# Attention's reciprocal row sums: through DRAM and back as one row, in place of diagonals and a product with ones

## The chip, the cores and the metric

One core of one Trainium2 chip runs the whole program, with its five engines: TensorE (PE), VectorE (DVE), ScalarE (ACT), GpSimd (POOL) and SyncE (SP), the last of which here only issues DMAs. The metric is the device time of one launch in microseconds. Three runs of the kernel before took 2953.47, 2957.74 and 2959.49 us; their median is 2957.74 us.

## What is computed

Two layers over x (2048 tokens of width 1024, float32). The even layer has a gated linear attention branch and a latent attention branch (MLA), the odd layer a gated MLP. The change touches only the end of MLA:

```
s = einsum('bqhd,bkhd->bhqk', qn_i, kn) + einsum('bqhr,bkr->bhqk', qr_i, kr)
p = softmax(s, axis=-1)
o = einsum('bhqk,bkhd->bqhd', p, v)
return o * silu(z)                 # 4 heads, 2048 queries, values of 128
```

The kernel doesn't divide p. It computes exp(s - max), multiplies by the values, and applies 1 / (row sum) together with silu(z) at the end. The values' product is held transposed (value dimension on partitions, queries along the free axis), so the 256 reciprocals of a pair of query tiles, computed as one number per partition, have to become a row that all 128 partitions hold.

## The kernel before, in words

MLA takes 4 heads x 16 tiles of 128 queries. A step I (32 of them) is a pair of tiles u = 0, 1; N = 2I + u numbers the tiles. All engines run the same sequence of steps written out by hand, with counting semaphores between them; nothing is reordered at run time.

- PE (`attn_pe`, L1767). `scores(N)` writes four banks of 512 keys, five matmuls each (L1775 to L1779). `turn(N, c)` transposes a quarter of exp(s) (8 transposes for two calls, L1786) and may write its bank only when DVE has read what the bank held before (the wait on `s_lo`). `values(I, c)` is 16 times a pair of matmuls (L1808, L1809). In step I, u = 0: scores of tile 2I with turns 0 and 1 of the tile before between banks 1 and 2, then turns 2 and 3, then the first half of the values of step I-1. For u = 1: the scores of tile 2I+1, with turns 0 and 1 of tile 2I between, then `shares(I-1)`, the second half of the values of step I-1, turns 2 and 3.
- DVE (`attn_dve`, L1944). Per tile: four maxima (L1947), their maximum (L1950), its negative times the scale (L1952, the tile `nm`), four low parts of the turned exp(s) (L1965), the row sum (L1958), its reciprocal (L1960, tile `rinv`), and one sum for the next layer's modulation (L1746), which reads a piece of `wmod` that SP loaded into `mw`. Once a step also `shared` (L1971), which multiplies the reciprocals' row into the gate tile `mzt`, and `outs` (L1977, L1978, L1980).
- ACT (`attn_act`). Four exponentials per tile (L1889, they wait for `nm`) and four high parts (L1896, they wait for the turns).
- POOL (`attn_pool`, L2046). `diagonal` makes diag(rinv) in three instructions (L2054, L2056, L2058); it waits for `rinv` and for `shares` of the step before. `query_split` (three instructions) then makes the parts of the queries two tiles ahead.
- SP (`attn_sp`). Per step: for each u the queries of two tiles ahead (L1445, L1447 twice; they wait for POOL's split), the `wmod` piece (L1738), then the store of the step before (L2084) and the gate tile (L2079).

`shares` on PE multiplies a matrix of ones with the high and the low part of the two diagonals, two matmuls of 256 columns into bank 7 (L1795, L1796); DVE reads the row from there. After the last step come the remaining turns, the modulation products (`mod1_pe`), the last `shares` and the last values; SP goes on with loads for the output projection.

Of the kernel before, what the change touches and what calls it, by code (L numbers as in the profile page):

```python
# [18 lines left out]
F32 = mybir.dt.float32  # L19
# [5 lines left out]
ds = bass.ds  # L25
# [42 lines left out]
def emit(nc, a, out):  # L68
# [5 lines left out]
    mixT = scratch("mixT", (KD, P, S))  # L74
    q_all = scratch("q_all", (P, MH * S))
    q_rot = scratch("q_rot", (ROPE, MH * S))
    x1 = scratch("x1", (S, D))
    gla_vs = scratch("gla_vs", (NT, P, GH * DV + 2 * DV))
    gla_a = scratch("gla_a", (NT, P, GH, P))
# [4 lines left out]
    with ExitStack() as ctx:  # L84
# [1563 lines left out]
        mvl = at("mvl", M0 + 32 * K, [P, MH, S], F32R)  # L1648
        pb_ = at("pb_", M0 + 111 * K, [P, 2, S])
        pt = at("pt", M0 + 127 * K, [P, NT, 2, 2 * P], F32R)  # L1650
        dgh = at("dgh", M0 + 64 * K, [P, 2, P], F32R)
        dgl = at("dgl", M0 + 65 * K, [P, 2, P], F32R)
        qraw = at("qraw", M0 + 68 * K, [P, 2, 2, P])
        qsl = at("qsl", M0 + 76 * K, [P, 2, 3, P], F32R)
        diag = at("diag", M0 + 168 * K, [P, 2, P])
        mzt = at("mzt", M0 + 169 * K, [P, 2 * P])
        ost = at("ost", M0 + 170 * K, [P, 2 * P])
        mx4 = at("mx4", M0 + 171 * K, [P, 2, 4])
# [40 lines left out]
        s_nm = sem("s_nm")  # L1699
        s_exp = sem("s_exp")  # L1700
        s_rinv = sem("s_rinv")
        s_dg = sem("s_dg")
        s_T = sem("s_T")
        s_hi = sem("s_hi")
        s_lo = sem("s_lo")
# [61 lines left out]
        def attn_pe(pe):  # L1767
# [19 lines left out]
                                      ident[:, :])  # L1787
                mm.then_inc(s_T, 1)

            def shares(I):  # L1790

                pe.wait_ge(s_dg, I * 6 + 12)
                pe.wait_ge(s_rz, I + 1)
                both = ones[:, :].bitcast(F32R)
                pe.matmul(PS[:, 7, 0:2 * P], both, dgh[:, :, :].rearrange("p u c -> p (u c)"), start=True, stop=False)  # L1795
                pe.matmul(PS[:, 7, 0:2 * P], both, dgl[:, :, :].rearrange("p u c -> p (u c)"), start=False, stop=True  # L1796
                          ).then_inc(s_rb, 1)

            def values(h, I, c):

                vh, vl = mvh[:, h, :], mvl[:, h, :]
# [10 lines left out]
            def step(h, i):  # L1812
                I = i + h * NP_
                first = isinstance(i, int) and i == 0
                opening = h == 0 and first
                hb = h - 1 if first else h
                for u in range(2):
                    N = i * 2 + (h * NT + u)

                    def turn_if(c):  # L1820
                        if u or not opening:
                            turn(N - 1, 1 - u, c)

                    def values_if(c):
                        if not opening:
                            values(hb, I - 1, c)

                    def pieces(*ns):
                        if opening:
                            for n in ns:  # L1830
                                piece_pe(pe, n)
                    if opening and u == 0:
                        pe.wait_ge(s_mor, NT - 1)
                        scores(h, N, u, (0,))
                        pieces(0, 1)
                        pe.wait_ge(s_mor, NT)
                        scores(h, N, u, (1,))
                        pieces(2)
                        pe.wait_ge(s_mgz, NT)
                    else:  # L1840
                        scores(h, N, u, (0, 1))
                    turn_if(0)
                    turn_if(1)
                    if u:
                        pieces(8, 9)
                    scores(h, N, u, (2,))
                    if u:
                        pieces(10, 11)
                    else:
                        pieces(3)  # L1850
                    scores(h, N, u, (3,))
                    if u == 0:
                        turn_if(2)
                        turn_if(3)
                        values_if(0)
                        values_if(1)
                        pieces(*range(4, 8))
                    else:
                        if not opening:
                            shares(I - 1)  # L1860
                        pieces(12, 13)
                        values_if(2)
                        values_if(3)
                        turn_if(2)
                        turn_if(3)
                        pieces(14, 15)
# [6 lines left out]
            for p in range(2):  # L1873
                for c in (2 * p, 2 * p + 1):
                    turn(MH * NT - 1, 1, c)
                if p:
                    mod1_pe(pe)
                    shares(MH * NP_ - 1)
                values(MH - 1, MH * NP_ - 1, 2 * p)
                if p:  # L1880
                    mod1_last(pe)
                values(MH - 1, MH * NP_ - 1, 2 * p + 1)
# [61 lines left out]
        def attn_dve(dve):  # L1944
# [7 lines left out]
                    dve.tensor_scalar(nm[:, u:u + 1], mx1[:, u:u + 1], rq2[:, 0, ds(i * 2 + u, 1)], -1.0, ALU.mult, ALU.mult  # L1952
                                      ).then_inc(s_nm, 1)

            def sums(N, u):
                dve.wait_ge(s_exp, N * 4 + 8)
                dve.wait_ge(s_dg, N * 3 + 1)
                dve.tensor_reduce(rsm[:, u:u + 1], rs4[:, u, :], AX, ALU.add).then_inc(s_rinv, 1)  # L1958
                dve.wait_ge(s_rinv, N * 2 + 1)
                dve.reciprocal(rinv[:, u:u + 1], rsm[:, u:u + 1]).then_inc(s_rinv, 1)  # L1960
# [5 lines left out]
                                  pt[:, o[0], 0, o[1]].bitcast(F32), ALU.subtract).then_inc(s_lo, 1)  # L1966

            def shared(I):
                dve.wait_ge(s_rb, I + 2)
                dve.wait_ge(s_mlg, I * 16 + 16)  # L1970
                dve.tensor_tensor(mzt[:, :], PS[:, 7, 0:2 * P], mzt[:, :], ALU.mult).then_inc(s_rz, 1)  # L1971

            def outs(I):
                dve.wait_ge(s_rz, I + 2)
# [7 lines left out]
            def step(h, i):  # L1982
                I = i + h * NP_
                opening = h == 0 and isinstance(i, int) and i == 0
                for u in range(2):
                    N = i * 2 + (h * NT + u)

                    def lo(c):
                        if u or not opening:
                            los(N - 1, 1 - u, c)  # L1990

                    def pieces(*ns):
                        if opening:
                            for n in ns:
                                piece_dve(dve, n)
                    maximum(N, i, u, 0)
                    if u == 0:
                        pieces(0, 1)
                    maximum(N, i, u, 1)
                    lo(0)  # L2000
                    lo(1)
                    if u:
                        pieces(8, 9)
                    else:
                        pieces(2)
                    maximum(N, i, u, 2)
                    if u == 0:
                        pieces(3)
                        maximum(N, i, u, 3)
                        lo(2)  # L2010
                        lo(3)
                        pieces(*range(4, 8))
                    else:
                        pieces(10, 11)
                        maximum(N, i, u, 3)
                        if not opening:
                            shared(I - 1)
                        pieces(12, 13)
                        if not opening:
                            outs(I - 1)  # L2020
                        lo(2)
                        lo(3)
                        pieces(14, 15)
                    sums(N, u)
                    mod1_sum(dve, h, i, u)
            heads(dve, step)
            for c in range(4):
# [18 lines left out]
        def attn_pool(pool):  # L2046
            def split(N, I, u):
                query_split(pool, N, I, u)

            def diagonal(N, I, u):  # L2050
                pool.wait_ge(s_rinv, N * 2 + 2)
                pool.wait_ge(s_rb, I + 1)
                pool.wait_ge(s_dg, N * 3 + 6)
                pool.tensor_tensor(diag[:, u, :], ident[:, :], rinv[:, u:u + 1].broadcast_to([P, P]), ALU.mult).then_inc(s_dg, 1)  # L2054
                pool.wait_ge(s_dg, N * 3 + 7)
                pool.tensor_tensor(dgh[:, u, :], diag[:, u, :], zero[:, 0:1].broadcast_to([P, P]), ALU.add).then_inc(s_dg, 1)  # L2056
                pool.wait_ge(s_dg, N * 3 + 8)
                pool.tensor_tensor(dgl[:, u, :], diag[:, u, :], dgh[:, u, :].bitcast(F32), ALU.subtract).then_inc(s_dg, 1)  # L2058

            mod1_start(pool)  # L2060
            with pool.Fori(0, MH * NP_ - 1) as I:
                for u in range(2):
                    diagonal(I * 2 + u, I, u)
                    split(I * 2 + 2 + u, I + 1, u)
            for u in range(2):
                diagonal(MH * NT - 2 + u, MH * NP_ - 1, u)

        def attn_sp(sp):
            for u in range(2):
# [7 lines left out]
            def gates(h, i, I):  # L2077
                sp.wait_ge(s_oe, I + 1)
                sp.dma_start(mzt[:, :], projT[h + T_MZ, :, ds(i * (2 * P), 2 * P)]  # L2079
                             ).then_inc(s_mlg, 16)  # L2080

            def store(h, i, I):
                sp.wait_ge(s_oe, I + 2)
# [3 lines left out]
            def step(h, i, last):  # L2087
# [8 lines left out]
                elif h:  # L2096
                    store(h - 1, NP_ - 1, I - 1)
                gates(h, i, I)
            mod1_rows(sp)
            for h in range(MH):  # L2100
                step(h, 0, False)
# [998 lines left out]
        def _(pool):  # L3100
# [6 lines left out]
            pool.sem_inc(s_q, 6)  # L3107
            main_pool(pool)

            pool.sem_inc(s_dg, 6)  # L3110
            attn_pool(pool)

            out_pool(pool, 0, lambda: (norm_pool_front(pool, 4), norm_pool_front(pool, 5)))
# [41 lines left out]
        def _(pe):  # L3155
# [4 lines left out]
            pe.sem_inc(s_S, 8)  # L3160
            pe.sem_inc(s_T, 8)
            pe.sem_inc(s_O, 4)
            pe.sem_inc(s_rb, 1)

            attn_pe(pe)

# [75 lines left out]
```

## Time and profile before

| | |
|---|---|
| median of three runs | 2957.74 us (2953.47 to 2959.49) |
| profiled execution: its own time, its span | 2955.36 us, 2953.6 us |
| mean granted TensorE clock | 0.988 |
| PE busy | 2878.6 us (97%) |
| DVE busy | 1597.1 us (54%) |
| ACT busy | 1351.9 us (46%) |
| POOL busy | 1101.2 us (37%) |
| MLA's 32 steps in the span | about 745 to 1360 us |

Busy is the share of time in which at least one instruction of the engine is in flight. Matmuls overlap, so on PE the distance from one start to the next says what a matmul costs, and "busy" doesn't show short waits. The span runs from the first to the last instruction; 1.8 us of the execution's time lie around it.

### The profile page before, as it was taken

What the parts mean: (1) busy time and instruction counts of PE and PEld (TensorE: products, weight loads), DVE (VectorE), ACT (ScalarE), POOL (GpSimd) and SP (SyncE); (2) the same over time, 40 slices, a digit from 0 to 9 for tenths busy, and PEclk for the clock granted to TensorE, in tenths of its full rate; (3) what the DMA queues carried; (4) which work ended last, traced back from release to release, by engine and by line L of the source; (5) the groups of instructions that cost most, each with busy time, mean ns of one, the idle gap of its engine ahead of it and who ended that gap; (6) DMA issues with size and microseconds to landing.
All of it is one profiled execution on the core that took longest, in us unless ns stands there. A gap on an engine that the chain in (4) does not pass through costs nothing.

```text
span 2953.6 us, 48956 instructions
## 1 busy us (share of the span) xinstructions
PE 2878.6 (97%) x16038; PEld 2398.2 (81%) x16038; DVE 1597.1 (54%) x2745; ACT 1351.9 (46%) x2444; POOL 1101.2 (37%) x1085
## 2 busy tenths in 40 slices
PE   7999999999999999999999999999999999999998
PEld 6768888788788888887877888888887888888887
DVE  5567777766777777773435222255557554532111
ACT  4652254565555555553235111265657665632111
POOL 0211111223233333332321762086766777623221
PEclk8999999989999999999999999999999999999999
DMA  7243355587111122123643332333235332244321
GB/s 282 61 131 102 103 164 159 164 286 255 59 57 55 56 57 57 57 58 134 192 163 122 136 150 85 103 126 103 96 103 185 108 103 99 99 158 150 104 95 57
DMA packets 279082, 356.88 MB, mean 121 GB/s; under 512 B 22116, under 2 KB 186084, under 8 KB 278407
## 3 DMA queue, kind: packets, MB, share of 16 engines
q1 hardware_dynamic: 273576, 339.45, 35.6%
q0 software_dynamic: 3072, 11.54, 1.0%
q10 hardware_dynamic: 2304, 4.20, 0.4%
q8 instruction: 77, 1.26, 0.2%
q14 instruction: 53, 0.43, 0.0%
HBM read 241.20 MB, written 111.80 MB: 120 GB/s over the span
## 4 chain that ended last, share of the span: by engine, by line
PE 87%; DVE 4%; ACT 3%; issue 2%; DMA 2%; POOL 1%; SPq 0%; DVEq 0%; ACTq 0%; POOLq 0%
PE PS L3028 6%; PE PS L3032 6%; PE PS L3036 6%; PE PS L2387 4%; PE PS L2389 4%; PE PS L2388 4%; PE PS L366 4%; PE PS L368 4%; PE PS L367 4%; PE PS L1808 4%; PE PS L1786 4%; PE PS L2555 4%; PE PS L2557 4%; PE PS L2556 4%; PE PS L1809 2%
## 5 line engine op out<-in xcount | busy, mean ns | idle before, releaser
L366 PE MATMUL PS<-hTh,whi 128*128 128x512 f32 x640 | 258.1, 403 | 1.5 <-DVE hTl L320 1.1
L3028 PE MATMUL PS<-hTh,wc 128*128 128x512 f32 x896 | 243.9, 394 | 8.0 <-DVE zu L2962 5.0
L368 PE MATMUL PS<-hTh,wlo 128*128 128x512 f32 x640 | 250.7, 392 | 0.0
L367 PE MATMUL PS<-hTl,whi 128*128 128x512 f32 x640 | 250.6, 392 | 0.0
L1889 ACT ACTIVATE pb__159<-PS,nm,rq 128x512 f32<-128x512 f32 x256 | 197.3, 779 | 106.5 <-DVE nm L1952 106.3
L2784 POOL TENSOR_TENSOR wc<-wpr,wc 128x512 fp32r<-128x512 f32 x128 | 176.9, 1382 | 179.3 <-ACT wc L2780 179.3
L3032 PE MATMUL PS<-hTh,wc 128*128 128x512 f32 x896 | 240.4, 390 | 0.0
L3036 PE MATMUL PS<-hTl,wc 128*128 128x512 f32 x896 | 239.8, 389 | 0.0
L2387 PE MATMUL PS<-ow_h,of_h 128*128 128x512 f32 x576 | 224.3, 389 | 1.4 <-DVE oy L2338 1.4
L2388 PE MATMUL PS<-ow_l,of_h 128*128 128x512 f32 x576 | 224.1, 389 | 0.0
L2389 PE MATMUL PS<-ow_h,of_l 128*128 128x512 f32 x576 | 224.1, 389 | 0.0
L2334 DVE SCALAR_TENSOR_TENSOR oy<-PS,small,gate 128x1024 f32<-128x1024 f32 x32 | 41.1, 1284 | 329.3 <-POOL small L2309 329.3
L1896 ACT ACTIVATE pt<-PS 128x512 fp32r<-128x512 f32 x256 | 139.4, 598 | 152.5 <-PE PS L1786 152.5
L2555 PE MATMUL PS<-vsh,hTh 128*128 128x512 f32 x512 | 199.8, 390 | 2.0 <-DVE vsl L2505 1.5
L3028 PEld LDWEIGHTS PS<-hTh,wc 128*128 128x128 f32 x896 | 165.9, 188 | 42.8 <-issue 10.3
L2557 PE MATMUL PS<-vsh,hTl 128*128 128x512 f32 x512 | 199.2, 389 | 0.0
L2556 PE MATMUL PS<-vsl,hTh 128*128 128x512 f32 x512 | 199.2, 389 | 0.0
L3032 PEld LDWEIGHTS PS<-hTh,wc 128*128 128x128 f32 x896 | 168.8, 188 | 35.4
L3036 PEld LDWEIGHTS PS<-hTl,wc 128*128 128x128 f32 x896 | 168.2, 188 | 35.6 <-DVE hTl L2728 0.6
L1808 PE MATMUL PS<-pt,mvh 128*128 128x512 f32 x512 | 185.8, 402 | 1.1 <-DVE pt L1965 1.1
L2054 POOL TENSOR_TENSOR diag<-ident,rinv 128x128 f32<-128x128 f32 x64 | 38.3, 598 | 395.6 <-PE PS L1796 284.1
L2301 POOL TENSOR_TENSOR of_l<-of,of_h 128x1024 fp32r<-128x1024 f32 (+1 forms) x24 | 84.4, 3517 | 240.2 <-ACT of_h L2262 240.2
(303 smaller groups left out, 7052.5 us busy)
## 6 DMA issues: line engine op xcount, KB each, us to landing
wpr<-wuz SPq DMA_DIRECT2D x128, 256.0 KB, 3.3
xt<-x SPq DMA_DIRECT2D x8, 2048.0 KB, 8.8
mw<-wmod SPq DMA_DIRECT2D x64, 256.0 KB, 2.7
oxt<-x SPq DMA_DIRECT2D x32, 512.0 KB, 4.9
sg_v<-vev SPq DMA_DIRECT2D x64, 256.0 KB, 2.4
vm<-sg_v SPq DMA_DIRECT2D x32, 512.0 KB, 3.8
sgT<-mT SPq DMA_DIRECT2D x32, 512.0 KB, 3.5
chnk<-pev SPq DMA_DIRECT2D x48, 256.0 KB, 2.7
```

The lines of the kernel that those rows point to most:

```text
L366: pe.matmul(PS[:, bank, :], w[1][:, s, k, :], hTh[:, k, b], start=(k == 0), stop=False)
L367: pe.matmul(PS[:, bank, :], w[1][:, s, k, :], hTl[:, k, b], start=False, stop=False)
L368: mm = pe.matmul(PS[:, bank, :], w[2][:, s, k, :], hTh[:, k, b], start=False, stop=(k == KD - 1))
L2387: pe.matmul(o, w["fh"][:, u, k, :], w["h"][:, k, c], start=(k == 0), stop=False)
L2388: pe.matmul(o, w["fh"][:, u, k, :], w["lo"][:, k, c], start=False, stop=False)
L2389: mm = pe.matmul(o, w["fl"][:, u, k, :], w["h"][:, k, c], start=False, stop=(k == OK[l] - 1))
L2555: pe.matmul(o, hTh[:, k, tok], vsh[:, k, :], start=(k == 0), stop=False)
L2556: pe.matmul(o, hTh[:, k, tok], vsl[:, k, :], start=False, stop=False)
L2557: mm = pe.matmul(o, hTl[:, k, tok], vsh[:, k, :], start=False, stop=(k == KD - 1))
L3028: pe.matmul(o, wc[:, k, 0, kk, :], h_tile(hTh, k, kk), start=(kk == 0 and not onto), stop=False, skip_group_check=onto)
L3032: pe.matmul(o, wc[:, k, 1, kk, :], h_tile(hTh, k, kk), start=False, stop=False, skip_group_check=onto)
L3036: mm = pe.matmul(o, wc[:, k, 0, kk, :], h_tile(hTl, k, kk), start=False, stop=(kk == 3), skip_group_check=onto)
```

## The change

POOL's `diagonal` and PE's `shares` go, with the tiles `diag`, `dgh`, `dgl`. SP stores `rinv` (128 partitions x 2 numbers) into a row of 256 numbers in DRAM, waits for that store, and loads the row into all 128 partitions of a new tile `share`. The row's order is (q u), so `shared` on DVE reads `share` with a step of two numbers. DVE's row sum waits until the store of the step before has read `rinv`.

```diff
+    rinvd = scratch("rinvd", (MH + 1, NT * P))
...
-        dgh = at("dgh", M0 + 64 * K, [P, 2, P], F32R)
-        dgl = at("dgl", M0 + 65 * K, [P, 2, P], F32R)
+        share = at("share", M0 + 64 * K, [P, 2 * P])
-        diag = at("diag", M0 + 168 * K, [P, 2, P])
...
-            def shares(I):
-                pe.wait_ge(s_dg, I * 6 + 12)
-                pe.wait_ge(s_rz, I + 1)
-                both = ones[:, :].bitcast(F32R)
-                pe.matmul(PS[:, 7, 0:2 * P], both, dgh[...], start=True, stop=False)
-                pe.matmul(PS[:, 7, 0:2 * P], both, dgl[...], start=False, stop=True).then_inc(s_rb, 1)
...
-                        if not opening:
-                            shares(I - 1)
...
-                    shares(MH * NP_ - 1)
...
-            def sums(N, u):
+            def sums(N, I, u):
                 dve.wait_ge(s_exp, N * 4 + 8)
-                dve.wait_ge(s_dg, N * 3 + 1)
+                if not isinstance(I, int) or I:
+                    dve.wait_ge(s_rst, I * 16)
...
             def shared(I):
-                dve.wait_ge(s_rb, I + 2)
+                dve.wait_ge(s_rb, I * 16 + 16)
                 dve.wait_ge(s_mlg, I * 16 + 16)
-                dve.tensor_tensor(mzt[:, :], PS[:, 7, 0:2 * P], mzt[:, :], ALU.mult).then_inc(s_rz, 1)
+                mz = mzt[:, :].rearrange("p (u q) -> p u q", u=2)
+                dve.tensor_tensor(mz, share[:, :].rearrange("p (q u) -> p u q", u=2), mz, ALU.mult).then_inc(s_rz, 1)
...
-            def diagonal(N, I, u):
...
                 for u in range(2):
-                    diagonal(I * 2 + u, I, u)
                     split(I * 2 + 2 + u, I + 1, u)
...
+            def row_shares(h, i, I):
+                sp.wait_ge(s_rinv, I * 4 + 4)
+                sp.dma_start(rinvd[h + 1:h + 2, ds(i * (2 * P), 2 * P)].rearrange("a (p u) -> p (a u)", u=2), rinv[:, :]).then_inc(s_rst, 16)
+                sp.wait_ge(s_rst, I * 16 + 16)
+                sp.dma_start(share[:, :], rinvd[h + 1:h + 2, ds(i * (2 * P), 2 * P)].broadcast_to([P, 2 * P])
+                             ).then_inc(s_rb, 16)
...
                 gates(h, i, I)
+                row_shares(h, i, I)
```

## Rows read from the trace of the kernel before

**Rows 1.** Busy time by stretch: us, busy and (count) of PE, PEld, DVE, ACT, POOL, PEclk, DMA share, GB/s

```profile
1000.00:1100.00 100.00, 100.00 (x572) 86.33 (x571) 75.77 (x162) 56.49 (x130) 32.18 (x66) 1.00 0.19 53
```

**Rows 2.** Timeline of PE around `shares`: start us, us, engine, line, operation

```profile
1002.04 0.29 PE L1795 MATMUL PS<-dgh,ones 128*128 128x256 f32 x1
1002.29 0.39 PE L1808 MATMUL PS<-pt,mvh 128*128 128x512 f32 x1
...
1020.60 0.29 PE L1795 MATMUL PS<-dgh,ones 128*128 128x256 f32 x1
```

**Rows 3.** Waits, 780 to 1330 us: who waited for whom, total us, times, longest

```profile
POOL diag L2054 <- PE PS L1796: 274.9, 30, 9.5
...
DVE ost L1977 <- PE PS L1809: 34.9, 27, 1.4
...
DVE mx L1947 <- PE PS L1779: 0.6, 3, 0.2
```

**Rows 4.** Timeline of DVE and ACT over one step

```profile
1003.28 0.22 DVE L1952 TENSOR_SCALAR nm<-mx,rq 128x1 f32<-128x1 f32 x1 [0.15 <-DVE mx L1950]
...
1006.95 0.80 ACT L1889 ACTIVATE pb__159<-PS,nm,rq 128x512 f32<-128x512 f32 x1
...
1007.97 0.16 DVE L1958 TENSOR_REDUCE rsm<-rs 128x1 f32<-128x4 f32 x1
...
1010.13 1.28 DVE L1965 TENSOR_TENSOR pt<-PS,pt 128x512 fp32r<-128x512 f32 x2
...
1011.32 1.28 DVE L1947 TENSOR_REDUCE mx<-PS 128x1 f32<-128x512 f32 x2
...
1012.93 0.21 DVE L1952 TENSOR_SCALAR nm<-mx,rq 128x1 f32<-128x1 f32 x1
...
1015.64 0.78 ACT L1889 ACTIVATE pb__159<-PS,nm,rq 128x512 f32<-128x512 f32 x1
...
1016.64 0.16 DVE L1958 TENSOR_REDUCE rsm<-rs 128x1 f32<-128x4 f32 x1 [2.30 <-ACT pb__159 L1889]
...
1017.12 0.75 DVE L1746 SCALAR_TENSOR_TENSOR macc<-mw,cvec,macc 128x512 f32<-128x512 f32 x1
...
1020.18 1.31 DVE L1947 TENSOR_REDUCE mx<-PS 128x1 f32<-128x512 f32 x2
...
1021.83 0.21 DVE L1952 TENSOR_SCALAR nm<-mx,rq 128x1 f32<-128x1 f32 x1 [0.15 <-DVE mx L1950]
```

**Rows 5.** Timeline of PE: turns 2 and 3 of the odd tile

```profile
1011.47 1.03 PE L1786 MATMUL PS<-ident,pb__159 128*128 128x128 f32 x8
```

**Rows 6.** Timeline of PE: three successive `shares`

```profile
1094.81 0.29 PE L1795 MATMUL PS<-dgh,ones 128*128 128x256 f32 x1
...
1113.44 0.29 PE L1795 MATMUL PS<-dgh,ones 128*128 128x256 f32 x1
...
1131.96 0.29 PE L1795 MATMUL PS<-dgh,ones 128*128 128x256 f32 x1
```

**Rows 7.** Timeline of SP's DMA issues after the end of a step's stores

```profile
1007.28 0.34 SPq L2079 DMA_DIRECT2D mzt<-projT  x1
1008.27 0.33 SPq L1445 DMA_DIRECT2D qraw<-q_all  x1
...
1010.17 0.34 SPq L1738 DMA_DIRECT2D mw<-wmod  x1
```

**Rows 8.** DMA issues, whole span: count, KB each, median us from issue to landing

```profile
mw<-wmod SPq DMA_DIRECT2D x64, 256.0 KB, 2.7
...
mixT<-og SPq DMA_DIRECT2D x16, 256.0 KB, 6.0
...
mixT<-ost SPq DMA_DIRECT2D x32, 128.0 KB, 2.3
```

**Rows 9.** Timeline of PE in the tail, around the last `shares`

```profile
1353.54 1.91 PE L1753 MATMUL PS<-maccg,ones 128*128 128x512 f32 x2
...
1355.46 0.42 PE L1796 MATMUL PS<-dgl,ones 128*128 128x256 f32 x1
```

More of the change, by code:

```diff
@@ L1701, in emit @@
         s_rinv = sem("s_rinv")
-        s_dg = sem("s_dg")
+        s_rst = sem("s_rst")
         s_T = sem("s_T")
@@ L1788, in turn @@
                 mm.then_inc(s_T, 1)
-            def shares(I):
-                pe.wait_ge(s_dg, I * 6 + 12)
-                pe.wait_ge(s_rz, I + 1)
-                both = ones[:, :].bitcast(F32R)
-                pe.matmul(PS[:, 7, 0:2 * P], both, dgh[:, :, :].rearrange("p u c -> p (u c)"), start=True, stop=False)
-                pe.matmul(PS[:, 7, 0:2 * P], both, dgl[:, :, :].rearrange("p u c -> p (u c)"), start=False, stop=True
-                          ).then_inc(s_rb, 1)
             def values(h, I, c):
@@ L2023, in step @@
                         pieces(14, 15)
-                    sums(N, u)
+                    sums(N, i + h * NP_, u)
                     mod1_sum(dve, h, i, u)
@@ L2048, in split @@
                 query_split(pool, N, I, u)
-            def diagonal(N, I, u):
[L2051 to L2058, printed above, removed]
             mod1_start(pool)
@@ L2062, in attn_pool @@
                 for u in range(2):
-                    diagonal(I * 2 + u, I, u)
                     split(I * 2 + 2 + u, I + 1, u)
-            for u in range(2):
-                diagonal(MH * NT - 2 + u, MH * NP_ - 1, u)
         def attn_sp(sp):
@@ L3108, in _ @@
             main_pool(pool)
-            pool.sem_inc(s_dg, 6)
             attn_pool(pool)
@@ L3162, in _ @@
             pe.sem_inc(s_O, 4)
-            pe.sem_inc(s_rb, 1)
             attn_pe(pe)
```

## The prediction, made before the changed kernel ran

> **What bounds the kernel now.** The page first: PE is busy 97% of the span, so an edit that takes two matmuls from each of 32 steps looks like a sure gain. The view by stretches says the same of the place where the edit lies: between 1000 and 1100 us PE is busy 100.00 of 100.00 us, DVE 75.77, ACT 56.49, POOL 32.18 [rows 1]. I don't stop there, because "busy" on PE hides waits shorter than a matmul's flight. The timeline gives PE's real pace: `shares` begins at 1002.04 and the next one at 1020.60, so a step lasts 18.56 us [rows 2].
>
> Then the view of waits. The striking thing is who does not wait: DVE's maxima read PE's scores, and in 550 us they waited for PE three times, 0.6 us in all [rows 3]. If PE alone set the pace, DVE would arrive early at every bank of scores. So I follow DVE and ACT through one step [rows 4]. `nm` of the odd tile starts at 1003.28. ACT's exponentials start from it, back to back with two high parts; the fourth runs at 1006.95, and its accumulator (which comes at the end) frees the row sum at 1007.97. From there DVE goes without a gap: reciprocal, the modulation sum, two maxima, low parts at 1010.13, two maxima at 1011.32, ending with `nm` of the even tile at 1012.93. From 1007.97 to 1012.93 these are eleven DVE instructions, first and last shown; each starts as the one before ends. Then again four exponentials, the fourth at 1015.64, row sum at 1016.64, modulation sum at 1017.12, maxima, low parts, maxima at 1020.18, `nm` at 1021.83. From `nm` to `nm` 18.55 us, the length of the step, and in that ring there is no place where PE is waited for but one: the last maximum at 1020.18 needs the fourth bank of scores. The pair there takes 1.31 us where the pair at 1011.32 takes 1.28. That is all the slack that the ring has: 0.03 us in 18.55.
>
> So two things bind at once: PE's queue at 18.56 and a ring of DVE and ACT at 18.53 that doesn't pass through what is removed. Where PE would meet the ring when it runs ahead: its turn 3 of the odd tile writes a bank that DVE must have read. DVE's low parts that read it end at 1010.13 + 1.28 = 1011.41; PE's turns start at 1011.47, eight of them within 1.03 us, the last ends included, so turn 3 comes near 1011.9 [rows 4, 5]. Less than 0.5 us of lead is open to PE.
>
> A second sign: `shares` at 1094.81, 1113.44 and 1131.96 are 18.63 and 18.52 apart [rows 6]. After a late step PE makes up 0.03 us and not more.
>
> **The change, part by part.**
>
> *PE loses two matmuls a step.* By starts they cost 1002.29 - 1002.04 = 0.25 us [rows 2]. 31 of the 32 stand inside the steps: 31 x 0.25 = 7.75 us of PE's queue. What the time gains is the smaller of this and what the ring allows: 31 x 0.03 = 0.93 us. The rest becomes lead of PE, used up after two steps (2 x 0.25 against at most 0.5), and then a wait of about 0.2 us per step at the turns. Lead that PE still has at the end of the last step buys nothing, because the turns of the last tile wait for the same ring. Bounds: 0 below, 7.75 above; I take 0.9.
>
> One rule speaks of this. The Trainium skill, page "Perfetto Trace Analysis", section "Identifying the Most-Contended Engine", says that matmul busy time doesn't measure how near TensorE is to its limit, and that weight-load busy should be looked at; the rows have 100.00 for the one and 86.33 for the other. By the first view the sum would be the whole 7.75, by the second PE isn't full, as the ring says.
>
> *The last shares* stands in the tail, where PE works without waiting between `mod1_pe` and the last values. `mod1_pe` ends at 1353.54 + 1.91 = 1355.45 and L1796 at 1355.46 + 0.42 = 1355.88 [rows 9]: 0.43 us at most, and 0.25 at the pace of the steps. I take 0.3. DVE's last `shared` gets its row earlier than before; the output's chain still starts from the last values.
>
> *POOL loses six instructions a step.* It waited 274.9 us for PE [rows 3]; nobody waits for POOL in the steps. The query splits come earlier. Worth nothing: bounds 0 and 0.
>
> *DVE's `shared`* reads `share` from SBUF with a step of two numbers instead of PSUM. It runs between `nm` and `outs`, and before `outs` DVE waits for PE's values by 1.3 us (34.9 / 27) [rows 3]. If the read took twice as long, that would still cover it. `nm` is issued ahead of it. Nothing. The row itself arrives some 3 us after the store's landing, where DVE needs it half a step later. The row sum's new wait, for the store of the step before, was met more than half a step earlier, and takes the place of a wait on `s_dg`: nothing.
>
> *SP gets a store, a wait for it, and a load, at the end of each step.* This is the part that can cost. Behind the wait stand, in SP's order, the queries of tile 2I+4 and the `wmod` piece for the even tile. The reciprocals are ready at 1007.97 + 0.16 + 0.16 and gaps = 1008.33; the store issues 0.2 us later, 1008.5. It lands L later; 0.2 more, and the row's load issues at 1008.7 + L. From one issue to the next across the loop's end took 1008.27 - 1007.28 = 0.99 us, and from there to the `wmod` load 1010.17 - 1008.27 = 1.90 [rows 7]. The piece lands 2.7 us after its issue [rows 8]: 1008.7 + L + 0.99 + 1.90 + 2.7 = 1014.3 + L. DVE's modulation sum at 1017.12 [rows 4] has to have it at about 1017.0, and that sum is in the ring. So L may be 2.7 us. The nearest row, `mixT<-ost` with 128 KB, took 2.3 [rows 8]; the new store has 1 KB, in 128 pieces of 8 bytes, and goes behind the gate tile's load in the queue. I take 2.0 to 2.3: margin 0.4 to 0.7 us, cost nothing. The farthest store has 6.0 (`mixT<-og`), as the upper bound. The queries have a whole step of time, and the odd tile's `wmod` piece half a step.
>
> *After the last step* SP's first loads of output weights go out some 3 us later. PE comes to them only behind its last turns, the modulation products and the last values, which start after 1355.88 [rows 9], while SP's loads follow the last reciprocals, ahead of all these: covered, worth nothing.
>
> **Sum.** 0.9 + 0.3 = 1.2 us less. The profiled execution took 2955.36 us and would take 2954.2; it stands 2.38 us below the median, so against the median 2957.74 - 1.2 = 2956.5 us. What a measurement can tell from no change is about 0.2%, 5.9 us.
>
> **The rivals.**
>
> *PE's queue alone sets the pace.* Then 31 x 0.25 + 0.3 = 8.1 us go: 2949.6. For it: PE never shows a wait, 100.00 busy. Against it: the 0.6 us of DVE's waits, and the ring closed in [rows 4]. It would need PE to be ahead at the turns by more than it is. Chance 0.13.
>
> *The `wmod` piece comes late (slower).* If L is over 2.7 us, DVE's modulation sum waits in each step, the ring is longer by L - 2.7, and PE waits with it: 31 x (L - 2.7). With L = 3.1: +12.4 - 0.3, 2969.8; with L = 6.0: +102, 3060. For it: the store is followed by a dependent load on one queue, and margins of half a microsecond rest on medians; the broadcast load lies ahead of the `wmod` load. Against: 1 KB is less than any store in the rows. The Trainium skill, page "DMA: Bandwidth & Descriptors", section "Anatomy of one DMA — SWDGE (gpsimd) path", warns that waiting for a completed write can cause "a surprisingly long delay especially when the write target is HBM"; a fixed cost of about 2.0 us stands there, an estimate by which L would lie inside the margin. Chance 0.19, about 0.05 of it with a loss under 0.2%.
>
> *The ring gets shorter*, because POOL's accesses no longer lie beside DVE's and ACT's. Up to PE's new length, so at most the first rival's time; no row shows DVE slower beside POOL. Chance 0.03.
>
> The forecast has 0.65. Faster by over 0.2%: the 0.13 of the first rival and 0.02 for the third and the spread, 0.15. Slower by over 0.2%: 0.14 of the second and 0.02 for the spread, 0.16. The rest, 0.69, is no difference that can be told. The likeliest case's own range is 2953.5 to 2960, mostly the spread of the runs. The whole range goes to 2949 below and 2966 above.
>
> **What would show it.** Right: steps of 18.52 to 18.54 us between equal PE instructions; late starts of PE at L1786, turn 3 of the odd tile; PE busy no longer 100% in the steps; DVE's `nm` to `nm` unchanged; the modulation sum still right behind the reciprocal in even tiles. Steps of 18.3 us would show the first rival. A wait of DVE's modulation sum for the DMA `mw<-wmod`, and a store of `rinv` that lands later than 2.7 us, would show the second. My forecast is wrong if the ring has slack that I took for work, for one if a step gets clearly shorter than 18.5 us.

## The result, and the profile after

The changed kernel takes 2964.07 us in the median of 20 runs (2958.76 to 2973.49); beside it the kernel before took 2956.14 us in 20 runs (2948.93 to 2962.15). The medians are 7.9 us apart; the ratio is 1.0025, with a 95% interval of 1.0019 to 1.0032, which is 7.4 us slower. Where I say below how many us a kernel gained or lost in time, the figure is worked out from its ratio in the same way, unless I say that it is of steps. I had forecast 1.2 us faster and called it no difference. The time lies inside the range, but on the side of the slower rival, to which I gave 0.19.

The profiled execution of the changed kernel took 2958.76 us, the fastest of its 20. Its span is 2957.0 us, 3.4 more than before. The steps of MLA, from the first `nm` of the phase to the last (from the trace, starts of L1952 and of L1939), took 596.09 us against 591.92, 4.17 more. The rest is -0.8: 1.76 more ahead of the first `nm`, where nothing was changed, 0.69 less from the last `nm` to the output projection, 1.83 less behind that. The parts that the change doesn't touch differ by several us between the profiled executions of the kernels below: the first `nm` comes at 744.5 to 751.1 us, and from the output projection to the end it takes 1588.7 to 1595.8. So I compare the steps; each comparison of them rests on one execution of each kernel.

Busy time by stretch of the kernel after, columns as in [rows 1]. PE, full before, now has short waits:

```profile
1000.00:1100.00 100.00, 99.90 (x555) 83.42 (x554) 74.56 (x159) 56.17 (x128) 19.42 (x34) 1.00 0.28 67
```

The waits of the kernel after, 780 to 1330 us (who waited for whom, total us, times, longest):

```profile
PEld PS L1785 <- DVE pt L1953: 16.4, 70, 0.6
...
DVE macc L1745 <- DMA mw<-wmod: 7.9, 14, 1.4
...
DVE maccg L1745 <- DMA mw<-wmod: 2.5, 6, 0.8
```

None of the three lines exists before the change. The modulation sum waits for its `wmod` piece in 20 steps, always in the even tile, 10.4 us in all (`macc` is its accumulator in the first three heads, `maccg` in the fourth; some 0.13 us of each wait is there in steps without a late piece too), and PE's turns wait for DVE's low parts behind it. SP's own waits in the same stretch show what the piece stands behind:

```profile
SPq L2062 <- DMA rinvd<-rinv: 71.7, 29, 3.4
```

SP stood 2.5 us in each step at the store. The DMA issues of the kernel after in that stretch (count, KB each, median us to landing):

```profile
mw<-wmod SPq DMA_DIRECT2D x58, 256.0 KB, 2.8
...
share<-rinvd SPq DMA_DIRECT2D x29, 128.0 KB, 4.1
...
rinvd<-rinv SPq DMA_DIRECT2D x29, 1.0 KB, 2.9
```

The store of 1 KB takes 2.9 us, where the stores of 128 KB in the steps took 2.3 before [rows 8] and 2.5 at most. One late step, as DVE's timeline of the kernel after has it, with the SP issues that belong to it in the second fence. The reciprocal of the odd tile is ready at 1012.38; the store goes out 0.18 later, the row's load after 2.88 more, the queries after 1.02 more, the piece after 1.97 more. In the kernel before the same piece went out at 1010.17, 1.8 us after the reciprocals [rows 7]; now it is 6.0 us.

```profile
1007.45 0.21 DVE L1939 TENSOR_SCALAR nm<-mx,rq 128x1 f32<-128x1 f32 x1 [0.15 <-DVE mx L1937]
...
1010.78 1.29 DVE L1953 TENSOR_TENSOR pt<-PS,pt 128x512 fp32r<-128x512 f32 x2 [1.08 <-ACT pt L1883]
1012.03 0.16 DVE L1946 TENSOR_REDUCE rsm<-rs 128x1 f32<-128x4 f32 x1
1012.22 0.16 DVE L1948 RECIPROCAL rinv<-rsm 128x1 f32<-128x1 f32 x1
...
1016.99 0.21 DVE L1939 TENSOR_SCALAR nm<-mx,rq 128x1 f32<-128x1 f32 x1
...
1020.89 0.17 DVE L1948 RECIPROCAL rinv<-rsm 128x1 f32<-128x1 f32 x1
1021.35 0.75 DVE L1745 SCALAR_TENSOR_TENSOR macc<-mw,cvec,macc 128x512 f32<-128x512 f32 x1 [0.30 <-DMA mw<-wmod]
...
1026.04 0.21 DVE L1939 TENSOR_SCALAR nm<-mx,rq 128x1 f32<-128x1 f32 x1 [0.15 <-DVE mx L1937]
```

```profile
1012.56 0.36 SPq L2060 DMA_DIRECT2D rinvd<-rinv  x1
1015.44 0.33 SPq L2062 DMA_DIRECT2D share<-rinvd  x1
1016.46 0.33 SPq L1446 DMA_DIRECT2D qraw<-q_all  x1
...
1018.43 0.34 SPq L1737 DMA_DIRECT2D mw<-wmod  x1
```

There is a second thing in the first fence. From `nm` of the odd tile to `nm` of the even one, a half step in which no piece is late, it takes 9.54 us, where the kernel before took 9.65 [rows 4]. The changed kernel's steps without a late piece took 18.44 us at most, where most steps before took 18.46 to 18.55. The experiments have to part the two.

### The profile page after: what moved, and what is told of

Read it like the earlier page. It is cut to its first block, busy times and chain, and to the rows that moved or that the text cites. A ratio compares the mean times of both kernels' runs of the same rounds, so it can differ in the third digit from the quotient of the medians.

```text
span 2957.0 us, 48518 instructions
## 1 busy us (share of the span) xinstructions
PE 2879.1 (97%) x15974; PEld 2386.4 (81%) x15974; DVE 1599.5 (54%) x2745; ACT 1354.5 (46%) x2444; POOL 1018.7 (34%) x893
## 4 chain that ended last, share of the span: by engine, by line
PE 86%; DVE 5%; ACT 3%; issue 2%; DMA 2%; SPq 1%; POOL 0%; ACTq 0%; DVEq 0%; POOLq 0%
PE PS L3012 7%; PE PS L3016 7%; PE PS L3020 7%; PE PS L2371 4%; PE PS L2373 4%; PE PS L2372 4%; PE PS L367 4%; PE PS L369 4%; PE PS L368 4%; PE PS L2539 4%; PE PS L2541 4%; PE PS L2540 4%; PE PS L1798 3%; PE PS L1785 3%; PE PS L3037 2%
## 5 line engine op out<-in xcount | busy, mean ns | idle before, releaser
L2026 POOL TENSOR_TENSOR qsl<-qraw,zero 128x256 fp32r<-128x256 f32 x64 | 39.9, 623 | 467.4 <-DMA qraw<-q_rot 301.5
L1953 DVE TENSOR_TENSOR pt<-PS,pt 128x512 fp32r<-128x512 f32 x256 | 163.7, 680 | 32.8 <-ACT pt L1883 32.8
```

## The experiments

Theory 1: SP's wait for the store makes the even tile's `wmod` piece late, and the modulation sum lies in the ring of DVE and ACT that sets the pace. Theory 2: the added traffic costs, wherever it stands. Theory 3: the loss comes from what was removed. Each kernel ran beside the kernel before on the same chip; the ratio is to that. The three sets of experiments ran on three different chips, so times are compared across sets by their ratios.

### Four kernels that part the three theories

**split** leaves everything in and changes SP's order alone. The wait and the row's load come behind the even tile's queries and its `wmod` piece:

```diff
                 for u in range(2):
                     if not last:
                         query(I * 2 + 2 + u, u)
                     mod1_load(sp, h, i, u)
+                    if u == 0:
+                        if not isinstance(i, int) or i:
+                            row_load(h, i - 1, I - 1)
+                        elif h:
+                            row_load(h - 1, NP_ - 1, I - 1)
...
-                row_shares(h, i, I)
+                row_store(h, i, I)
```

> The changed kernel with its parts in another order on SP: the store of the reciprocals is issued as before, but the wait for it and the row's load come in the next step, behind the even tile's queries and wmod piece, so nothing that the next tile needs stands behind the wait. Theory 1 (the wait on SP makes the even tile's wmod piece late, and DVE's modulation sum waits for it in the ring of DVE and ACT): the sum's waits for mw<-wmod (10.7 us, 21 times in the changed kernel) go to about 0, all steps take 18.40 to 18.50 us, and the time is 2 to 5 us under the kernel before. Theory 2 (what costs is the added traffic itself, 128 reads of one row and 128 pieces of 8 bytes, wherever it stands): the same traffic, so still 5 to 10 us over the kernel before. Theory 3 (the loss comes from what was removed, the query splits now falling elsewhere): as theory 2, 5 to 10 us over.

2948.72 us (9 runs), ratio 0.9971, interval 0.9961 to 0.9981: 8.6 us under the kernel before (the medians are 9.5 apart). SP's issues in the split order; the piece goes out before the row's load:

```profile
1008.23 0.35 SPq L2060 DMA_DIRECT2D rinvd<-rinv  x1
1009.27 0.33 SPq L1446 DMA_DIRECT2D qraw<-q_all  x1
...
1011.24 0.34 SPq L1737 DMA_DIRECT2D mw<-wmod  x1
1012.25 0.33 SPq L2064 DMA_DIRECT2D share<-rinvd  x1
```

No wait of the sum for `mw<-wmod` is left. The steps took 586.76 us in all, the median one 18.43. The same bytes move and the same work is removed, so theories 2 and 3 fall as I put them; that traffic costs when it stands ahead of the piece is not excluded by this run. The changed kernel's steps are 9.3 us longer than these, and its sum waited 10.7 us in all of the phase, in 21 steps: without the 0.13 us that is there anyway some 8 us (an estimate). The two are of one size. The gain in time was larger than the 2 to 5 us that I expected; 5.2 us of it lie in the steps, the rest outside them, and no run says why.

**none** has no round trip: no store, wait or load, and `share` is a tile of ones. With the store goes the wait that DVE's row sum had for it.

```diff
+            pool.memset(share[:, :], 1.0).then_inc(s_rb, 1)
...
-                if not isinstance(I, int) or I:
-                    dve.wait_ge(s_rst, I * 16)
...
-                row_shares(h, i, I)
```

> Left out: the reciprocals' way to a row. There is no store, no wait and no load, the row is a tile of ones set once; PE's two matmuls and POOL's diagonals stay removed. Theory 1: nothing delays the wmod piece; steps of 18.40 to 18.50 us as in the split order, 2 to 5 us under the kernel before, not the 8 us that PE's queue lost, because the ring of DVE and ACT holds. Rival (PE's queue alone sets the pace): steps of 18.30 us, 8 us under. Theory 3: 5 to 10 us over the kernel before.

2948.43 us (6 runs), ratio 0.9966 (0.9954 to 0.9978). The steps took 584.25 us, the median one 18.33: neither the 18.40 to 18.50 of theory 1 nor clearly the 18.30 of PE's queue. This was a miss, and it asked for the second set. The round trip in the split order, with the row sum's wait that belongs to it, costs 2.5 us of steps against none at all; none_wait below says which of the two it is.

**both** is the kernel before with SP's store, wait and load put in, and nothing removed. DVE's row sum gets the wait for the store as a third one, behind its two others.

```diff
                 dve.wait_ge(s_dg, N * 3 + 1)
+                if not isinstance(I, int) or I:
+                    dve.wait_ge(s_rst, I * 16)
...
                 gates(h, i, I)
+                row_shares(h, i, I)
```

Nobody reads the row that it loads.

> The kernel before with diagonals, matmuls and POOL's work all kept, and SP's store, wait and load of the row added in the place where the change has them; nobody reads the loaded row. Theory 1: the wmod pieces come late as in the changed kernel; since this kernel has no lead of PE to spend and a longer step, 5 to 13 us over the kernel before, with waits of the modulation sum for mw<-wmod of about 5 to 12 us. Theory 3: no change, within 2 us.

2967.52 us (6 runs), ratio 1.0037 (1.0025 to 1.0050), 11 us slower; its steps took 603.77 us, 11.9 more than before. The sum's waits in it:

```profile
DVE macc L1749 <- DMA mw<-wmod: 9.1, 15, 2.4
...
DVE maccg L1749 <- DMA mw<-wmod: 3.7, 6, 1.8
```

So the round trip makes a loss without anything being removed. Not all of the 11.9 us is lateness, though. This is a step without a late piece, from one odd tile's `nm` to the next, 18.62 us, where the same step of the kernel before took 18.47:

```profile
780.55 0.22 DVE L1955 TENSOR_SCALAR nm<-mx,rq 128x1 f32<-128x1 f32 x1
...
799.17 0.21 DVE L1955 TENSOR_SCALAR nm<-mx,rq 128x1 f32<-128x1 f32 x1
```

Its other steps without a late piece took 18.61 us in the first head and 18.68 or 18.69 in the later ones (one where a head ends, 18.23), where the kernel before mostly has 18.46 and 18.55. What the ring of DVE and ACT has more in such a step is the row sum's third wait. At 0.13 to 0.15 us a step it makes about 4 us (an estimate for 31 steps), and the late pieces the other 8.

**distinct** loads a gate tile's 128 rows into `share` where the change reads one row 128 times.

```diff
-                sp.dma_start(share[:, :], rinvd[h + 1:h + 2, ds(i * (2 * P), 2 * P)].broadcast_to([P, 2 * P])
+                sp.dma_start(share[:, :], projT[h + T_MZ, :, ds(i * (2 * P), 2 * P)]
                              ).then_inc(s_rb, 16)
```

> The changed kernel, but the load after the wait reads 128 different rows of 1 KB (a gate tile) in place of one row 128 times; the result's scale is wrong for it. The row's load took 4.1 us in the median, gate tiles of the same size 2.7. Theory 1: the store and its wait delay the wmod piece as before, only the traffic ahead of it gets shorter: between 2 and 8 us over the kernel before, the sum's waits for mw<-wmod 5 to 11 us. Theory 2 (reading one row 128 times holds up the queue): load lands in about 2.7 us, the wmod waits vanish, and the time is at or under the kernel before.

2959.96 us (11 runs), ratio 1.0008 (0.9999 to 1.0017). The load lands in 2.4 us in place of 4.1, the waits are 7.3 + 2.5 = 9.8 us in the profiled execution. The waits stay, as theory 1 has it. The ratios (1.0008 against 1.0025) suggest that the repeated row adds something too, while the profiled executions hardly differ (steps 594.51 against 596.09). How much it adds isn't settled by this.

### Four kernels on what sets the pace of a step

In the kernel before DVE's sequencer takes the wait for the last exponential, then computes the register for the row sum's second wait, 46 ns, and only then can start the row sum. This is the view by line of L1957, the wait on `s_dg` in `sums` (DVEq is DVE's sequencer, under which the trace lists DVE's waits and register operations):

```profile
L1957 DVEq FUSED_REGOPS  x56: 46/46/46, 775.7 to 1342.1; - x56
```

In the changed kernel and in split the second wait, for `s_rst`, is in 34 of 62 cases an event alone. In the pair of tiles of split that I followed, the odd tile's row sum (1007.71) starts 0.02 us behind the exponential's signal and the even tile's (1016.38), with the register, 0.12 behind it; in the kernel before it is 0.12 for both. Two of the rows of L1945 in split (the third is 7 more registers):

```profile
L1945 DVEq EVENT_SEMAPHORE  x34: 21/21/21, 786.8 to 1338.0; - x34
L1945 DVEq FUSED_REGOPS  x21: 46/46/46, 924.0 to 1328.8; - x21
```

**split_swap** exchanges the two waits in the split order.

```diff
-                dve.wait_ge(s_exp, N * 4 + 8)
                 if not isinstance(I, int) or I:
                     dve.wait_ge(s_rst, I * 16)
+                dve.wait_ge(s_exp, N * 4 + 8)
```

> The split order, with the row sum's two waits on DVE exchanged: first the one on the store of the step before (met long ago), then the one on the last exponential. In the clean steps of the kernel before, DVE computes a register of 46 ns and then starts the row sum 0.09 us after the exponential's signal; in the split order that is so for one of the two tiles (steps of 18.43 us), in the kernel without the round trip for neither (18.33 us). Ring theory (the pace of a step is the length of the ring of DVE and ACT, and PE's queue at 18.31 us lies just under it): steps go from 18.43 to 18.33 us, 3 us less than the split order. Rival (PE's queue or something in the traffic set the 18.43 us): steps stay at 18.43.

The median step is 18.34 us, as expected. Two odd tiles' `nm` of split and then of split_swap, 18.43 and 18.35 us apart:

```profile
1003.12 0.21 DVE L1939 TENSOR_SCALAR nm<-mx,rq 128x1 f32<-128x1 f32 x1 [0.15 <-DVE mx L1937]
...
1021.55 0.21 DVE L1939 TENSOR_SCALAR nm<-mx,rq 128x1 f32<-128x1 f32 x1 [0.15 <-DVE mx L1937]
```

```profile
1000.96 0.21 DVE L1939 TENSOR_SCALAR nm<-mx,rq 128x1 f32<-128x1 f32 x1 [0.15 <-DVE mx L1937]
...
1019.31 0.21 DVE L1939 TENSOR_SCALAR nm<-mx,rq 128x1 f32<-128x1 f32 x1 [0.15 <-DVE mx L1937]
```

All steps together took 585.40 us, 1.4 less than split, not 3. About 1 us of what is missing lies in six steps in a row of the third head, which took 18.45 to 18.73; none_wait and the kernel before have such longer steps in the same place (18.54 and 18.59 or more), split, none and before_short don't, and I don't know the cause. The time doesn't show the gain: 2950.33 us (11 runs), ratio 0.9979 (0.9970 to 0.9989) against split's 0.9971. As a gain in time it is a miss, or too small to be seen.

**none_wait** puts a wait behind the row sum's wait in none; it is met long before.

```diff
                 dve.wait_ge(s_exp, N * 4 + 8)
+                if not isinstance(I, int) or I:
+                    dve.wait_ge(s_S, I * 8)
```

> The kernel without the round trip (left out: the reciprocals' way to a row, a tile of ones stands in), with one wait added back behind the row sum's wait for the exponential, on a count of PE's that is met long before. Ring theory: the register and wait in the ring give back 0.09 to 0.20 us a step, from 18.33 to between 18.42 and 18.53 us, 3 to 6 us more than without it. Rival (DMA traffic made the difference between 18.33 and 18.43): stays at 18.33.

2951.53 us (10 runs), ratio 0.9985 (0.9976 to 0.9994). None has 0.9966, so by the ratios it is 5.6 us over none; the two intervals leave about 1 to 10 us. The median step is 18.43, the steps together 587.84, 3.6 more than none. There is no row's traffic in this kernel. So the 0.10 us between 18.33 and 18.43 is one wait's work in DVE's sequencer, not DMA. That is also what split has over none (18.43 against 18.33, 2.5 us of steps): in the split order I can see no cost of the round trip's traffic in the steps.

**before_short** cuts the even tiles' modulation sum in the kernel before from 512 columns to 8.

```diff
+            n = 512 if u else 8
-            dve.scalar_tensor_tensor(acc, mw1[:, u, :], cvec[:, ds(i, 1)], acc, ALU.mult, ALU.add).then_inc(s_macc, 1)
+            dve.scalar_tensor_tensor(acc[:, 0:n], mw1[:, u, 0:n], cvec[:, ds(i, 1)], acc[:, 0:n], ALU.mult, ALU.add).then_inc(s_macc, 1)
```

> The kernel before with DVE's modulation sum of the even tiles cut to 8 of its 512 columns (that part of the next layer's modulation is left out), which takes some 0.5 us out of the ring of DVE and ACT. PE's queue, 18.55 us with its two extra matmuls, stays. If the kernel before was held by both to within 0.03 us: steps stay at 18.52 to 18.55 us and the time within 1 us of the kernel before. If DVE and ACT alone held it, steps fall by up to 0.5 us and the time by up to 15 us.

The median step is 18.55 us, within a nanosecond that of the kernel before; together 591.78 against 591.92. DVE now waits for PE's scores more often:

```profile
DVE mx L1948 <- PE PS L1780: 1.4, 6, 0.3
```

So PE's queue did hold the kernel before at 18.55, with the ring close under it. The time was 2960.34 us (12 runs), ratio 1.0017 (1.0006 to 1.0028): a little slower, although the steps are the same. In the profiled execution 4.7 us more lie behind the start of the output projection. I don't know why; it stays open.

**split_pool** moves the modulation sums to POOL, in the split order. POOL's loop over the steps is written out for it.

```diff
-            dve.scalar_tensor_tensor(acc, mw1[:, u, :], cvec[:, ds(i, 1)], acc, ALU.mult, ALU.add).then_inc(s_macc, 1)
+            dve.tensor_tensor(mw1[:, u, :], mw1[:, u, :], cvec[:, i:i + 1].broadcast_to([P, 512]), ALU.mult).then_inc(s_const, 1)
+            dve.wait_ge(s_const, i * 2 + (h * NT + u + 49))
+            dve.tensor_tensor(acc, mw1[:, u, :], acc, ALU.add).then_inc(s_macc, 1)
...
-                    mod1_sum(dve, h, i, u)
...
-            with pool.Fori(0, MH * NP_ - 1) as I:
...
+                    mod1_sum(pool, h, i, u)
+            for h in range(MH):
+                for i in range(NP_):
+                    step(h, i, h * NP_ + i == MH * NP_ - 1)
```

(`dve` is the name of the function's argument; it is now called with POOL.)

> The split order with the modulation sums of all tiles moved from DVE to POOL, as a product and an add of 512 columns each (about 1.4 us each, 5.6 us a step of POOL's 15 free). That takes some 1.3 us out of the ring of DVE and ACT, and a late wmod piece no longer meets it. Both theories of pace: PE's queue is left alone, steps of 18.31 us, 3.5 us less than the split order, some 12 us under the kernel before. It would be slower than that if POOL's two reads of SBUF slow DVE's low parts or ACT.

2948.12 us (9 runs), ratio 0.9971 (0.9962 to 0.9981). The median step is 18.25 us, the steps together 582.62, the shortest of all. PE is busy 100.00 of 100.00 us again between 1000 and 1100 us, so I take this for PE's queue without `shares`: 18.55 - 18.25 = 0.30 us a step, where [rows 2] gave 0.25. The time was to be some 12 us under the kernel before and is 8.6 under it, a miss: it equals that of split, and the 4 us of steps don't show in it. In the profiled execution its first `nm` comes 3.8 us later than in split and the part behind the output projection is 2.3 longer; whether POOL's written-out loop has to do with it was not tried. Split and split_pool are both about 8.6 us faster than the kernel before and 16 faster than the changed one; between the two I see no difference.

### Two kernels on the size of the lateness

**one_row** keeps order and wait and loads the row into one partition. The other 127 partitions hold ones.

```diff
-                sp.dma_start(share[:, :], rinvd[h + 1:h + 2, ds(i * (2 * P), 2 * P)].broadcast_to([P, 2 * P])
-                             ).then_inc(s_rb, 16)
+                sp.dma_start(share[0:1, :], rinvd[h + 1:h + 2, ds(i * (2 * P), 2 * P)]).then_inc(s_rb, 16)
```

> The changed kernel with the row's load after the wait cut from 128 partitions (128 KB) to one (1 KB); the shares used are ones, so the result's scale is wrong. SP's order and its wait for the store are as in the changed kernel, the wmod piece is issued about 5.8 us after the reciprocals, but no traffic lies in front of it. If the wait alone decides: the piece still lands in 2.6 to 2.8 us, at the edge of the 8.7 us that the sum leaves; sum's waits for mw<-wmod 3 to 8 us in total, time 0 to 4 us over the kernel before. If the row's load in front of the piece is what makes it late: waits near 0, steps of 18.43 us, and 5 to 9 us under the kernel before.

2958.11 us (11 runs), ratio 1.0008 (0.9999 to 1.0017); steps 590.91 us, waits:

```profile
DVE macc L1746 <- DMA mw<-wmod: 4.2, 7, 1.2
...
DVE maccg L1746 <- DMA mw<-wmod: 0.6, 1, 0.6
```

4.8 us of waits where the changed kernel has 10.4. About half of the lateness is the wait alone, the other half comes with the 128 KB that lie in front of the piece in the queue. The piece is only some 0.2 us earlier for it: it lands after 2.68 us in place of 2.78 in the median, and the row's load takes 0.08 less to issue. So near the edge 0.2 us decides about half of the waits. What remains is mostly the store's scatter: six of the eight waits of the sum follow a store that took 3.2 to 3.9 us to land. In the changed kernel, too, four of the five waits over 0.8 us do, with 3.4 to 3.9.

**mid** is the split order with the row's load one place earlier, ahead of the even tile's piece. The edit is shown against the changed kernel; `row_store` and `row_load` are as in split.

```diff
                         query(I * 2 + 2 + u, u)
+                    if u == 0:
+                        if not isinstance(i, int) or i:
+                            row_load(h, i - 1, I - 1)
+                        elif h:
+                            row_load(h - 1, NP_ - 1, I - 1)
                     mod1_load(sp, h, i, u)
```

> Between the changed kernel and the split order: the wait for the store and the row's load come in the next step behind the even tile's queries but ahead of its wmod piece. The queries' 2 us of issuing then overlap the store's flight, and the piece goes out about 3.7 us after the reciprocals in place of 5.8. Theory 1 (lateness against the 8.7 us decides): 2 us of margin, no waits of the sum, steps of 18.43 us, the time of the split order within 2 us, 8 us under the kernel before. If any piece that is issued behind the row's load is slowed (contention): some waits of the sum remain, and 2 to 6 us are lost against the split order.

2953.15 us (12 runs), ratio 0.9991 (0.9983 to 1.0000), steps 589.15. Three waits of the sum are left:

```profile
DVE macc L1745 <- DMA mw<-wmod: 2.6, 3, 1.2
```

The piece went out 4.9 us after the reciprocals, not 3.7, because with the three DMAs of the queries issued behind it the store takes 4.0 us to land and not 2.9 (in the three late steps 4.5 to 5.4); and the even tile's piece itself lands after 3.3 us in the median and 4.2 at most (5.0 in the last step). This is the second outcome that I had written down, with a loss of 2.4 us of steps against split.

Among the kernels with `shares` removed and the round trip in, the order by waits is the order by steps: waits of 0, 2.6, 4.8, 9.8 and 10.4 us go with steps of 586.8, 589.2, 590.9, 594.5 and 596.1 us.

## Why the prediction was wrong

*What bounds the kernel before*: right. PE's queue at 18.55 us and the ring of DVE and ACT just under it, both within 0.03 us. before_short shows the first: 0.5 us less in the ring changed nothing. For the second, what was put into the ring in none_wait, 0.10 us, came out in the step; that the ring of the kernel before was at 18.53 is worked out from this and split's 18.43, and fits.

*PE loses two matmuls a step*: my 0.9 us was too small. I took the ring's length as given, and put the new wait in the place of the one on `s_dg` at nothing. It isn't: in half of the tiles no register is computed for it behind the last exponential's signal, and the ring is 0.10 us shorter, 18.43 us. Without lateness the steps gain 5.2 us (split), not 0.9. The price of the two matmuls was small as well, 0.25 us a step against 0.30. The first rival's 7.75 us is what the steps of none gained (7.7), with one wait in the row sum; split_pool has 9.3.

*The last `shares`*: 0.3 us taken. Between the last `nm` and the output projection there are 0.69 us less, but the same stretch takes 24.2 to 28.6 us in the other kernels without `shares` and 23.3 in before_short, which has them. So the term isn't shown.

*POOL, and DVE's read of `share`*: nothing, as said, as far as the steps show. The instruction with the read takes 0.44 us in the mean against 0.42 with PSUM.

*SP's store, wait and load*: this is the step that failed. I put its cost at nothing, because the store would land in L = 2.0 to 2.3 us and up to 2.7 was free. The chain and its limit were right to within 0.2 us: 0.2 to the store, 0.99 and 1.90 behind it (measured 0.18, 1.02 and 1.97). From the store's landing to the row's issue I had 0.2 where the trace has 0.02, and from the piece's landing to the sum it has 0.21 where I left 0.1; with these the limit is about 2.8 (an estimate). The term that was mis-sized is L. I took it from a store of 128 KB and argued that 1 KB can't take longer; it took 2.9 us in the median, 2.6 to 3.9. And I put medians on both sides of an edge: besides L, the even tile's piece landed after 2.9 us at most in the kernel before, in the changed kernel after up to 3.6, six times after more than 3.0 (in the last step, where no queries are issued between the row's load and the piece, after 4.8). The second rival's formula, 31 x (L - 2.7), gives 6.2 us with L = 2.9, and about 3 with the limit of 2.8; 10.4 us of waits were seen, so most of it is the scatter, which none of my terms had.

In sum, the steps of the profiled executions lose 9.3 us by lateness (split to the changed kernel) and gain 5.2 by what was removed (the kernel before to split): +4.2. The two errors have opposite signs, and the time lies inside my range by that luck, not by the mechanism. The medians are 7.9 us apart, which is more than the +3.4 of the profiled spans: the profiled execution is the fastest of the changed kernel's 20, and the others are up to 15 us longer. Whether their lateness is larger no trace shows.

The sentence of the Trainium skill that I cited, on the page "DMA: Bandwidth & Descriptors", section "Anatomy of one DMA — SWDGE (gpsimd) path", warned of just this wait; the trace has 2.9 us beside its fixed cost of about 2.0, which that section gives for DMAs issued from GpSimd, while SP issued this store. I used the figure to lower the rival's chance, and should have used the warning.

## What to carry to other kernels

A round trip through DRAM that nothing needs for half a step can still cost, by what stands behind its wait in the issuing queue. Here it paid to issue the store, then the loads that the next tile needs, and only then to wait (split against the changed kernel). Where two engines' loops are within 0.03 us of each other, count each wait's register in the ring, and look for margins by the slowest landing of a queue, not the median. Where a ring of other engines is as long as PE's queue, what is taken off that queue shortens the step only as far as the ring gets shorter too.

## What the runs showed of the hardware

- A store of 1 KB, 128 partitions with 8 bytes each, took 2.9 us to land in the changed kernel, a store of 128 KB in 1 KB pieces 2.1 to 2.4 in the medians of these kernels. With the three DMAs of the queries (mid) or these and the piece (split) issued right behind it, the small store took 4.0 and 3.9 us. So DMAs that were issued later delayed one that was already under way.
- Reading one row of 1 KB 128 times took 4.1 us (changed kernel), 128 different rows 2.4 (distinct), in the same place of the same queue. The repeated row had also just been written; the runs don't part the two. In the split order the same read took 3.4.
- Whether a wait cost DVE 0.10 us a step or nothing depended on which of two waits stood first, where the one that is met long ago needs a register computed: 18.43 us in split, 18.34 in split_swap.
